# Moving the low rows of two fp32r operand buffers behind their high rows, and shifting both buffers by 64 bytes

## What is computed

```
h = h + attention(norm(h) @ w_qkv) @ w_o
h = h + square(relu(norm(h) @ w1)) @ w2
proj = norm(h) @ w_in
h = h + (g_a * y_a + g_b * (... @ conv_out_w)) @ w_o_2
h = h + (silu(gate) * up) @ w_down        # gate, up = norm(h) @ w_gate_up
```

## Time and profile before

| | |
|---|---|
| median of 3 runs | 2592.11 us (2592.04 to 2592.31) |
| the profiled execution | 2592.15 us, its span 2590.4 us |
| TensorE busy | 2580.2 us of 2590.4 |
| TensorE's weight loads busy | 2321.9 us |
| VectorE / ScalarE / GpSimd busy | 1614.6 / 1174.1 / 141.4 us |
| granted TensorE clock | 0.999 |
| mean DMA rate | 187 GB/s |

### The profile page before, as it was taken

One profiled execution on the slowest core, in us unless ns is written; L12 is line 12 of the kernel. 1 busy time (PEld: TensorE's weight loads), 2 busy tenths in 40 slices (PEclk: granted clock), 3 DMA queues, 4 the chain that ended last, 5 costly groups with the idle time before them and its releaser, 6 DMA issues.

```text
span 2590.4 us, 40378 instructions
## 1 busy us (share of the span) xinstructions
PE 2580.2 (100%) x16053; PEld 2321.9 (90%) x16053; DVE 1614.6 (62%) x1398; ACT 1174.1 (45%) x1181; POOL 141.4 (5%) x87
## 2 busy tenths in 40 slices
PE   9999999999999999999999999999999999999998
PEld 9999998888888888899899988888888888888887
DVE  6577766655556556886654776566756545554555
ACT  5455554434434444544533344444544434443444
POOL 0000100000000000000200530000000000000001
PEclk9999999999999999999999999999999999999999
DMA  7554455655655565555555555555555555555563
GB/s 263 180 171 157 162 182 191 193 186 190 195 190 185 192 195 189 184 179 186 188 181 189 182 181 193 188 186 194 194 184 190 181 192 194 189 190 191 191 211 130
DMA packets 243954, 485.26 MB, mean 187 GB/s; under 512 B 7728, under 2 KB 8944, under 8 KB 243696
## 3 DMA queue, kind: packets, MB, share of 16 engines
q1 hardware_dynamic: 243520, 483.12, 57.2%
q10 hardware_dynamic: 320, 0.53, 0.1%
HBM read 481.53 MB, written 2.10 MB: 187 GB/s over the span
## 4 chain that ended last, share of the span: by engine, by line
PE 99%; DVE 1%; issue 0%; ACT 0%; POOL 0%; DVEq 0%; POOLq 0%; ACTq 0%
PE ps L1327 42%; PE ps L1334 21%; PE ps L1374 14%; PE ps L1355 8%; PE ps L1382 7%; PE ps L1361 4%; PE ps L1430 0%; PE ps L1484 0%; PE ps L1396 0%; PE ps L1418 0%; PE ps L1257 0%; PE ps L1267 0%; PE ps L1489 0%; PE ps L1467 0%; PE ps L1421 0%
## 5 line engine op out<-in xcount | busy, mean ns | idle before, releaser
L771 DVE TENSOR_TENSOR wlo<-raw,whi 128x1024 fp32r<-128x1024 f32 x900 | 1107.8, 1262 | 923.9 <-ACT whi L564 923.8
L564 ACT ACTIVATE whi<-raw 128x1024 fp32r<-128x1024 f32 x900 | 919.3, 1054 | 1328.3 <-PE ps L1334 893.9
L1327 PE MATMUL ps<-b_buf,whi 128*128 128x512 f32 x2688 | 643.7, 392 | 0.0
L1327 PEld LDWEIGHTS ps<-b_buf,whi 128*128 128x128 f32 x2688 | 492.9, 188 | 97.6
L1334 PEld LDWEIGHTS ps<-b_buf,wlo 128*128 128x128 f32 x2688 | 334.9, 188 | 14.0
L1334 PE MATMUL ps<-b_buf,wlo 128*128 128x256 f32 x2688 | 337.9, 278 | 0.0
L1374 PE MATMUL ps<-a_buf,whi 128*128 128x258 f32 (+4 forms) x2560 | 330.9, 282 | 0.0
L1374 PEld LDWEIGHTS ps<-a_buf,whi 128*128 128x128 f32 x2560 | 315.7, 188 | 0.5 <-ACT a_buf L581 0.2
L1327 PE MATMUL ps<-c_buf,whi 128*128 128x512 f32 x1280 | 306.6, 392 | 0.0
L1327 PEld LDWEIGHTS ps<-c_buf,whi 128*128 128x128 f32 x1280 | 234.7, 188 | 46.4
L1327 PE MATMUL ps<-a_buf,whi 128*128 128x512 f32 x768 | 185.9, 394 | 0.0
(11 more groups left out here) (202 smaller groups left out, 1473.0 us busy)
## 6 DMA issues: line engine op xcount, KB each, us to landing
raw<-in_mlp_w_dram SPq DMA_DIRECT2D x128, 1024.0 KB, 5.2
raw<-in_w_in_dram SPq DMA_DIRECT2D x96, 1024.0 KB, 5.0
raw<-in_w_gate_up_dram SPq DMA_DIRECT2D x88, 1024.0 KB, 5.0
raw<-in_sb_w_qkv_dram SPq DMA_DIRECT2D x44, 1024.0 KB, 5.1
raw<-in_w_down_dram SPq DMA_DIRECT2D x44, 1024.0 KB, 5.1
raw<-in_sb_w_o_dram SPq DMA_DIRECT2D x16, 1024.0 KB, 5.1
raw<-in_conv_out_w_dram SPq DMA_DIRECT2D x16, 1024.0 KB, 5.1
raw<-in_w_o_dram SPq DMA_DIRECT2D x16, 1024.0 KB, 5.1
```

What stands on the lines that cost most here:

```text
L564: act.activation(whi[:, unit_of(n, u)], raw[:, n % RAW, u * UK:(u + 1) * UK, :], ACT.Copy).then_inc(w_hi, 1)
L771: dve.tensor_tensor(wlo[:, s], raw[:, n % RAW, u * UK:(u + 1) * UK, :], cast(whi[:, s]), ALU.subtract).then_inc(w_lo, 1)
L1327: pe.matmul(ps[:, 4 * half + j, :].rearrange("p (a n) -> p a n", a=2), whi[:, s, kt, j * P:(j + 1) * P], buf[:, :, x, tok], start=c == 0 a ...
```

## The change

`b_buf` and `c_buf` become `[P, NT, 2, T]`: in each, the 256 high values of a tile row are followed at once by its 256 low values. `c_buf` begins at the start of `a_buf`, and the 64 bytes ahead of `b_buf` are gone, so B and C begin at phase 0, and with B everything placed behind it moves by 64 bytes. The views `b_hi`, `b_lo`, `c_hi`, `c_lo` follow, and so do the writes of ScalarE and VectorE into them: the same number of values, as four runs of 256 with a step of 2048 bytes. For B and C the moving operand of L1327 is now one run of 512 values, and its output one run of 512 columns of a bank. A and D stay as they are. No instruction is added or removed.

```diff
-        c_buf, _ = place("c_buf", [P, 2, NT, T], F32R, at=a_off + 64)
+        c_buf, _ = place("c_buf", [P, NT, 2, T], F32R, at=a_off)
         d_buf, _ = place("d_buf", [P, 2, NT, T], F32R, at=a_off)
-        top[0] += 64
-        b_buf, b_off = place("b_buf", [P, 2, NT, T], F32R)
-        a_hi, a_lo, b_hi, b_lo = a_buf[:, 0], a_buf[:, 1], b_buf[:, 0], b_buf[:, 1]
-        c_hi, c_lo, d_hi, d_lo = c_buf[:, 0], c_buf[:, 1], d_buf[:, 0], d_buf[:, 1]
+        b_buf, b_off = place("b_buf", [P, NT, 2, T], F32R)
+        a_hi, a_lo, b_hi, b_lo = a_buf[:, 0], a_buf[:, 1], b_buf[:, :, 0], b_buf[:, :, 1]
+        c_hi, c_lo, d_hi, d_lo = c_buf[:, :, 0], c_buf[:, :, 1], d_buf[:, 0], d_buf[:, 1]
...
-            bufs = {"A": (a_buf, M), "B": (b_buf, 0), "C": (c_buf, 0), "D": (d_buf, 0)}
+            parts = {"A": (a_hi, a_lo, M), "B": (b_hi, b_lo, 0), "C": (c_hi, c_lo, 0), "D": (d_hi, d_lo, 0)}
+
+            def both(src, x):
+
+                if src == "A":
+                    return a_buf[:, :, x, M:TW]
+                return {"B": b_buf, "C": c_buf}[src][:, x].rearrange("p a n -> p (a n)")
+
+            def bank(src, b):
+
+                return ps[:, b, :].rearrange("p (a n) -> p a n", a=2) if src == "A" else ps[:, b, :]
...
-                buf, off = bufs[p.src]
-                hi, lo = buf[:, 0], buf[:, 1]
+                hi, lo, off = parts[p.src]
...
-                            pe.matmul(ps[:, 4 * half + j, :].rearrange("p (a n) -> p a n", a=2),
-                                      whi[:, s, kt, j * P:(j + 1) * P], buf[:, :, x, tok],
+                            pe.matmul(bank(p.src, 4 * half + j), whi[:, s, kt, j * P:(j + 1) * P], both(p.src, x),
                                       start=c == 0 and u == 0 and kt == 0, stop=False, skip_group_check=True)
...
-                              b_buf[:, :, t, P:T], start=False, stop=False, skip_group_check=True)
+                              b_buf[:, t, :, P:T], start=False, stop=False, skip_group_check=True)
```

## The result

The changed kernel takes **2606.39 us** (2606.25 to 2606.75, five runs) against 2592.26 for the kernel before (five runs beside them): a ratio of 1.0054, interval 1.0043 to 1.0065. It is 14.1 us slower, where 23 us less had been forecast.

A forecast was written before the change was run, and what follows sets the result against it. TensorE, almost never waiting, was taken as the bound, so only matmul pace could change: 19.2 + 4.3 - 0.2 = 23.3 us off 2592.15 gives 2568.8 us. The 8-in-10 range was 2566 to 2593.

The forecast's parts named there:

- Step 1: Paired chunks of B and C: 248 chunks at 5.440 instead of 5.518 us, 19.2 us less, 8.5 from 256-column matmuls.
- step 2: Unpaired products of B (`w_o`, `pw`): 40 units at 2.720 instead of 2.828 us, 4.3 us less.
- the two lossless paces: B and C after the change: 226.7 ns per 512-column and 113.3 ns per 256-column matmul, as no row is quicker.
- The term of 10.7 us: 512-column matmuls of paired B and C chunks: 3968 x 2.7 ns saved, 10.7 us less.
- without exception: Products of D: nine units of 12 512-column matmuls in 24.48 us, all at 226.7 ns.
- The bound named for the pace: Paired chunks: pace between 226.7 and 113.3 ns a matmul and A's 5.59 us a chunk.
- R2: Paired chunks: nothing measurable, 256-column matmuls all at 117.5 ns (2590 us) or phase without effect (2592 us); chance 0.12.
- R1: Paired chunks: only 512-column matmuls gain, the 256-column ones go on alternating; 10.7 us less, 2581.4 us; chance 0.13.
- Item 5: Buffers moved along with B: scores keep their relative offset; between 113.3 and 120 ns, 64 matmuls are worth 0.2 us, nothing.
- R3: Starts of matmuls: streams at equal phase collide, 248 chunks at A's 5.59 us, 17.9 us more, 2610 us; chance 0.15.
- Items 3 to 6: One run instead of two, four-run writes, buffers shifted with B, VectorE and ScalarE load: nothing extra, no new wait.
- The weighing of row against page: Pace of TensorE: measured rows differing by 2.7 ns a matmul were followed over the skill page saying TensorE never waits.

The follow-up runs named there:

- the last: Changed kernel, B and C at distance 64, own buffer for narrow-only products, 13th wide matmul split per paired chunk (four split in gu_1, gu_2): 2577.24 us, ratio 0.9941.
- run 6: Changed kernel with B and C at distance 192 and every paired product done by 256-column matmuls alone, 48 a chunk: 2588.13 us.

## Why the prediction was wrong

**Step 1 failed in its second half, and step 2 with it.** The prediction took "226.7 and 113.3 as the two lossless paces" and gave B and C both, as "both operands lie as D's and its weights do". D has 512-column matmuls alone. That its address relation is harmless at 256 columns too was carried over, not read from a row, and it is false: at distance 0 narrow matmuls settle at 120.0 ns. The 113.1 ns of B's better chunks, which seemed to bear it out, was one of two states at distance 64 and says nothing of distance 0. Instead of 8.5 us less (3968 x 2.0 ns are 7.9; 8.5 is what was left of the 19.2), the narrow ones of the paired chunks brought 15.7 more; instead of 4.3 less, the unpaired ones brought 2.1 more.

**The wide matmuls: right sign, wrong size.** 226.7 ns is reached, but only behind five slower matmuls, and each chunk starts anew behind its narrow ones: a mean of 228.5. The term of 10.7 us measured 3.6. D's own entry, which is uneven for five matmuls and takes 1.84 us for eight instead of 1.81, was in the trace of before: "without exception" is true of the nine units shown, not of D. Nine units in a row hide it, sixteen matmuls don't.

**The range left out the case that came.** The bound named for the pace, A's 5.59 us a paired chunk, does hold the 5.568 measured. But the range stopped at R2, with 117.5 as the slowest narrow pace. No row had 256 columns at phase 0, which R1 says in so many words, and still that pace was taken from rows at other phases. Item 5 had allowed 120 ns for the scores; the same allowance for the narrow matmuls here, 3968 x (120 - 115.3) + 960 x (120 - 117.8), would have been +20.8 us: 2602.3 beside the gain of the wide ones, 2613 without it. The upper end would have held the measurement.

**R3 came true in its sign; that it came near in size (2610 against 2606.4) is luck.** Its price was A's chunk, which is slow in the wide matmuls (3.71 us for 16) and has 1.88 in the narrow ones. Measured were 3.65 and 1.91, and by R3's own signs, 3.70 or more and a mean duration above 392 ns, it did not come (3.65, 391 ns). Its mechanism, two streams that begin at the same phase and harm one another, isn't shown either: wide matmuls have their best settled pace just there, and narrow ones take 120.0 ns on the mean at distance 96 too. Its chance of 0.15 was too small: "D loses nothing" was counted against it for all matmuls, and speaks for the wide ones only.

**Items 3 to 6 held.** One run instead of two: the layout alone is 1.0001. The writes:

```profile
L646 ACT ACTIVATE b_buf<-full 128x1024 f32 x20 | 20.9, 1046 | 0.0
L1063 DVE TENSOR_TENSOR b_buf<-full,b_buf 128x1024 f32 x20 | 24.4, 1221 | 0.0
```

1046 and 1221 ns, against 1046 and 1217 or 1218. The scores, with both operands shifted together, take 1.41 us for 12 instead of 1.40:

```profile
137.46 1.41 PE ps L1403 x12
```

The new wait of 0.3 us, for ScalarE at `a_buf`, is nothing. The weighing of row against page was right in its outcome, for an address alone moves the time by 14 us; the sign that I gave it was not.

**What stays open.** Why there are states at all, what a hiccup changes in them, and what sets the state at entry. The runs show that distance, width, order and what ran ahead decide, and that a kernel repeats its states (five executions of the last within 0.4 us). An account in the terms of the streams' meeting in memory fits, but no run took it apart.

## What to carry to other kernels

When TensorE is never kept waiting, its pace still depends on where the moving operand lies relative to the weights, at offsets within 256 bytes; judge an offset by matmuls of the very width that will use it, and for a stream of mixed widths by the mixture. Read it from starts, in the chain of waits, and look whether pieces with equal counts take equal times: an alternation like 1.81 and 1.88 is a state which the order of the matmuls can hold or lose. Of the seven offsets tried, the best for this mixture was already in place; the 15 us came from holding the quick state, by splitting one or four wide matmuls a chunk, and from giving the products of narrow matmuls alone an offset of their own. Look at every stretch by itself: no order tried was quick from every entry, and a stretch can be quick by a chance hiccup.

## What the runs showed of the hardware that was not expected

- Narrow matmuls have settled paces of 113.3, 117.8 and 120.0 ns on full clock and with no wait, and 116.7 at distance 32. The first two occur at one and the same pair of addresses (run 6).
- At distance 64 the last wide matmul tells the pace of all narrow ones behind it: quick behind 231 or 232 ns (123 chunks of 123), slow behind 225 to 229 (125 of 125).
- A change of width can cost: at distance 0 five wide matmuls of 228 to 236 ns pass before 226.7 is reached; with `wlo` 64 bytes off, ten (241, 238, 233, 236, 224, 231, 236, 228, 233, 230). At distance 64, in the quick state, it costs nothing: the wide ones begin with 226, 229, 232.
- Splitting a wide matmul costs nothing by itself: two narrow ones take 0.23 us, as much as one wide. More instructions (16469 instead of 16053 matmuls) made the quickest kernel.
- The quickest settled paces in any run are 226.7 and 113.3 ns. The page "TensorE: Matmul & The Clock Gate" of the Trainium skill (section "Back-to-back issue gap") gives N/2.4 + 2.5 ns for a single one on full clock; worked out from it, 215.8 and 109.2 here is an estimate, and no settled stretch of the fp32r matmuls in these runs came down to that.
